# Causal mask of a latent attention added by two 64 × 64 quadrant products instead of one 128 × 128 product

## The chip, the cores and the metric

The kernel runs on one core of a Trainium2 chip. The metric is the device time of one execution in microseconds (us), taken as the median of repeated runs. A core has TensorE (PE for matmuls, PEld for its weight loads), VectorE (DVE), ScalarE (ACT), GpSimd (POOL) and SyncE (SP), which run side by side and meet only at semaphores.

## What is computed

A chain of two transformer blocks on one sequence of 512 tokens by 1024 features. The part that matters here is one sublayer of the second block, a causal latent attention with 16 heads whose queries and keys have 96 features (64 plain, 32 rotated) and whose values have 64:

```python
Q_BLOCK, MLA_HEADS, QK_NOPE, QK_ROPE, V_HEAD = 128, 16, 64, 32, 64

def causal_block_attention(q, k, v, scale):
    ...
    def one_block(args):
        qi, n = args
        s = jnp.einsum('bhqd,bhkd->bhqk', qi, kt).astype(jnp.float32) * scale
        qpos = n * Q_BLOCK + jnp.arange(Q_BLOCK)
        s = jnp.where(kpos[None, :] <= qpos[:, None], s, -jnp.inf)
        p = jax.nn.softmax(s, axis=-1).astype(vt.dtype)
        return jnp.einsum('bhqk,bhkd->bqhd', p, vt)
```

Before it run two layers of another block (attention without a mask, a gated recurrence, a convolution, an MLP) and a gated MLP; after it a gated MLP, and a last layer with dilated attention between two more gated MLPs.

## The kernel before

All engines run programs written out by hand; nothing is scheduled by a tool, so the order of the source is the order on each engine. Weight matrices come in tiles by DMA, ACT copies each tile rounded (`split_hi`, L413), DVE subtracts to get the rest (`split_lo`, L422), and PE takes three products per tile (L444, L452 or L487): high by high, high by low, low by high.

The latent attention is woven into those projections. `mla_items` (L1923) makes the work list. For two heads at a time there are three pairs, one for query blocks 0 and 2 (key widths 128 and 384), one for block 3 (width 512), one for block 1 (width 256). Each of the two heads, called A and B below (y = 0 and 1), has its own PSUM bank, `banks[4]` and `banks[5]`. So a head pair has four score groups, in all 8 × 4 = 32 groups of two heads, and 64 masked products. `mla_at` (L1952) spreads the steps of the pairs over 17 points of each of four parts; a point lies between projection products of PE, and `weave` (L2022) runs there what is due. For one pair the steps are:

- **scores**, PE, `att_pe_step` (L849): waits for `p_ready` of the pair before (its banks are then read), then writes scores into banks 4 and 5 (L857). On top of the last 128 key columns of each group it adds the mask with a second product, an identity `EYE` by the table `CAUSAL` (L859); both are parts of the tensor `fixed`. The last product of a head counts up `s_ready`.
- DVE, `att_dve_step` (L913): for head A, then for head B, waits for `s_ready` and takes the row maximum of each group (L919), then its negative scaled (L921).
- ACT, `att_act_step` (L885): exponential with row sum for A, then for B (L893), which counts up `p_ready`.
- **divide**: DVE takes reciprocals (L928) and scales A (L933), ACT scales B (L902).
- **turn**: PE transposes the probabilities (L868), ACT copies them out (L910).
- **values**: PE multiplies by the values (L878), head A into partitions 0 to 63 and B into 64 to 127 of bank 3; for the last pair of two heads DVE stores the result (L951, L953).

In three of the parts the point 12 has `query_rope`: PE rotates queries (L1989) after all turned probabilities have been copied out of bank 6.

ACT also empties the projections' banks there (L2051, L2053, L2058, L2077). Tables and operands of scores, mask and values are float32, those of the projections are the rounded float32 form. In the profile a float32 product of the source appears as two PE records, and a rounded one as one.

In the profile's forms, 96\*128 means a stationary operand of 96 rows and 128 columns; 128\*64 one of 128 rows and 64 columns. The moving operand stands behind it.

Of the kernel before, what the change touches and what calls it, by code (L numbers as in the profile page):

```python
# [14 lines left out]
P = 128  # L15
# [13 lines left out]
HEAD = 64  # L29
# [173 lines left out]
def build(nc, io):  # L203
    ctx = ExitStack()
    with ctx:
# [28 lines left out]
        EYE, ONES, SWAP, FLIP, MSWAP, CAUSAL, REVERSE = (FIX[:, i * P:(i + 1) * P] for i in range(7))  # L234
# [30 lines left out]
        banks = [ctx.enter_context(nc.psum_tensor(f"bank{i}", [P, L], F32)) for i in range(8)]  # L265

        def line(name):
            return Line(ctx.enter_context(nc.semaphore(name)))
# [26 lines left out]
        for l in range(DEPTH):  # L295
            w = io["w_in"][l]
# [6 lines left out]
            w = io["w_out"][l]  # L303
# [20 lines left out]
        for i, s in steps2:  # L324
# [3 lines left out]
            elif i == 0:  # L328
                w = io["mla_w_in_2"][0]
# [5 lines left out]
                for part in range(4):  # L335
                    q = wq[:, 4 * QK * part:4 * QK * (part + 1)].rearrange("r (h c) -> r h c", c=QK)
# [7 lines left out]
            else:  # L344
                w = io["dil_w_in_2"][0]
# [11 lines left out]
        for u, unit in enumerate(units):  # L357
# [27 lines left out]
        s_ready, nmax_ready, p_ready, pn_ready, t_ready, pt_ready, pv_ready, o_used = (line(n) for n in (  # L385
            "scores_ready", "neg_max_ready", "probs_ready", "probs_normalised", "probs_turned", "probs_t_ready",
            "heads_out_ready", "heads_out_taken"))
# [461 lines left out]
        def att_pe_step(pe, pairs_, bufs, kind, i):  # L849
            if kind == "scores":  # L850
                pe.eng.wait_ge(p_ready.sem, p_ready.next(pe, 2, lag=2))
                both = pairs_[i]["items"]
                for n in range(len(both[0]["segs"])):
                    for y in range(2):
                        q, k, c0, add = both[y]["segs"][n]
                        b, w = banks[4 + y], k.shape[-1]
                        mm = pe.eng.matmul(b[:, c0:c0 + w], q, k, start=True, stop=add is None)  # L857
                        if add is not None:
                            mm = pe.eng.matmul(b[:, c0 + w - P:c0 + w], EYE, add, start=False, stop=True)  # L859
                        if n == len(both[0]["segs"]) - 1:  # L860
                            mm.then_inc(s_ready.sem, s_ready.add())
            elif kind == "turn":
                pair, y = divmod(i, 2)
                normal = pn_act if y else pn_ready
                pe.eng.wait_ge(normal.sem, normal.next(pe))
                pe.eng.wait_ge(pt_ready.sem, pt_ready.next(pe, lag=1 if i > 2 * bufs["one"] else 2))
                for j in range(pairs_[pair]["n"] // P):
                    mm = pe.eng.transpose(turn_bank(bufs, pair, y)[:, j * P:(j + 1) * P], bufs["pr"][i % 4][:, j * P:(j + 1) * P], EYE)  # L868
                mm.then_inc(t_ready.sem, t_ready.add())
            elif kind == "values":  # L870
                pe.eng.wait_ge(pt_seen.sem, pt_seen.next(pe, 2))
                if pairs_[i]["opens"]:
                    pe.eng.wait_ge(o_used.sem, o_used.next(pe, lag=1))
                both = pairs_[i]["items"]
                for j in range(len(both[0]["v"])):
                    for y in range(2):
                        v, c0, start, stop = both[y]["v"][j]
                        mm = pe.eng.matmul(banks[3][HEAD * y:HEAD * y + HEAD, c0:c0 + P], v, turned_probs(bufs, i, y)[:, j * P:(j + 1) * P], start=start, stop=stop)  # L878
                mm.then_inc(pv_ready.sem, pv_ready.add())

        def turned_probs(bufs, pair, y):

            return bufs["pt"][y + (2 if pair >= bufs["late"] else 0)]
# [61 lines left out]
        def turn_bank(bufs, pair, y):  # L945

            return banks[2 if y and pair < bufs["one"] else 6]
# [97 lines left out]
        def mixer_pe_step(pe, l, items, step):  # L1045
# [29 lines left out]
            elif kind in ("scores", "turn", "values"):  # L1075
# [4 lines left out]
                if (kind, i) == ("values", 0):  # L1080
                    for u, j in ((z_units(l)[0], 1), (lin[("z0", l)][-1], 1)):
                        place, turn = acc_place[units[u]["tiles_at"] + j]
                        pe.eng.wait_ge(acc_free[place].sem, turn)
                att_pe_step(pe, items, gqa_bufs, kind, i)
            elif kind == "csum":
                if i == 0:
# [1752 lines left out]
```

## Time and profile before

| | |
|---|---|
| median of 3 runs | 3885.82 us (3884.37 to 3890.31) |
| the profiled execution's own time | 3884.11 us |
| its span from first to last instruction | 3882.3 us |
| PE busy | 3676.9 us, 95% |
| DVE busy | 2141.2 us, 55% |
| ACT busy | 1350.1 us, 35% |
| mean granted TensorE clock | 0.967 |
| the latent attention's stretch | about 1868 to 2032 us of the span |

Times in the rows are microseconds from the start of the span. A row of the timeline has start, length, engine, line, operation, tensors and forms; like instructions that follow each other are merged, and xN says how many records a row holds. In brackets stands how long the engine had been idle before, and what ended that wait. Ends of matmuls are modelled: a record of a 128-column float32 product shows some 0.27 us, though the next begins 0.11 us after it, so starts are compared, not ends.

### The profile page before, as it was taken

What the parts mean: (1) busy time and instruction counts of PE and PEld (TensorE: products, weight loads), DVE (VectorE), ACT (ScalarE), POOL (GpSimd) and SP (SyncE); (2) the same over time, 40 slices, a digit from 0 to 9 for tenths busy, and PEclk for the clock granted to TensorE, in tenths of its full rate; (3) what the DMA queues carried; (4) which work ended last, traced back from release to release, by engine and by line L of the source; (5) the groups of instructions that cost most, each with busy time, mean ns of one, the idle gap of its engine ahead of it and who ended that gap; (6) DMA issues with size and microseconds to landing.
All of it is one profiled execution on the core that took longest, in us unless ns stands there. A gap on an engine that the chain in (4) does not pass through costs nothing.

```text
span 3882.3 us, 48060 instructions
## 1 busy us (share of the span) xinstructions
PE 3676.9 (95%) x19016; PEld 2966.1 (76%) x19016; DVE 2141.2 (55%) x2923; ACT 1350.1 (35%) x1795; POOL 854.0 (22%) x688
## 2 busy tenths in 40 slices
PE   8888999988899999998899999999999999989999
PEld 6567888756788878887677888788878778777887
DVE  5977444487844454347567435643574554655334
ACT  4554323256332332222673222222233333332212
POOL 2200655320055526552213630000000000000000
PEclk9999999999899999998899999999999999999999
DMA  5211655421155546563224643233322122222331
GB/s 158 64 39 47 156 146 147 103 63 47 44 147 146 147 117 152 143 146 76 62 63 101 157 125 98 73 102 97 98 74 84 61 74 74 60 66 76 98 98 65
DMA packets 564250, 377.76 MB, mean 97 GB/s; under 512 B 37297, under 2 KB 561162, under 8 KB 564026
## 3 DMA queue, kind: packets, MB, share of 16 engines
q1 hardware_dynamic: 564026, 374.69, 36.6%
q8 instruction: 151, 2.47, 0.3%
q14 instruction: 73, 0.60, 0.1%
HBM read 372.45 MB, written 2.17 MB: 96 GB/s over the span
## 4 chain that ended last, share of the span: by engine, by line
PE 77%; DVE 16%; ACT 4%; issue 2%; SPq 0%; DMA 0%; ACTq 0%; DVEq 0%
PE bank L444 61%; PE bank L452 2%; DVE conv_sum L1228 2%; PE bank L487 2%; DVE w_lo L422 2%; PE bank L481 1%; DVE std L919 1%; PE bank L482 1%; PE bank L857 1%; DVE hgrn_scores L1408 1%; DVE norm_tmp L1665 1%; DVE norm_tmp L1659 1%; ACT w_hi L413 1%; DVE X L1661 1%; PE bank L2291 1%
## 5 line engine op out<-in xcount | busy, mean ns | idle before, releaser
L444 PE MATMUL bank<-H_hi,w_hi 128*128 128x512 f32 x2384 | 968.8, 406 | 5.0 <-DVE w_lo L422 1.8
L444 PE MATMUL bank<-H_hi,w_lo 128*128 128x512 f32 x2384 | 932.0, 391 | 0.0
L444 PE MATMUL bank<-H_lo,w_hi 128*128 128x512 f32 x2384 | 931.4, 391 | 0.0
L422 DVE TENSOR_TENSOR w_lo<-w_raw,w_hi 128x2048 fp32r<-128x2048 f32 (+3 forms) x285 | 663.0, 2326 | 168.0 <-ACT w_hi L413 159.2
L413 ACT ACTIVATE w_hi<-w_raw 128x2048 fp32r<-128x2048 f32 (+3 forms) x285 | 529.1, 1856 | 308.5 <-DMA w_raw<-in_ffn_w_up 131.4
L520 POOL TENSOR_TENSOR w_mod_raw<-w_mod_raw,silu_c 128x1024 f32<-128x1024 f32 x144 | 282.8, 1964 | 1344.7 <-DMA w_mod_raw<-in_w_mod 1299.4
L444 PEld LDWEIGHTS bank<-H_hi,w_hi 128*128 128x128 f32 x2384 | 448.6, 188 | 141.1 <-issue 50.0
L444 PE MATMUL bank<-U_hi,w_hi 128*128 128x512 f32 x1376 | 540.7, 393 | 3.8 <-DVE note L963 3.8
L444 PE MATMUL bank<-U_hi,w_lo 128*128 128x512 f32 x1376 | 536.1, 390 | 0.0
L444 PE MATMUL bank<-U_lo,w_hi 128*128 128x512 f32 x1376 | 536.1, 390 | 0.0
L444 PEld LDWEIGHTS bank<-H_hi,w_lo 128*128 128x128 f32 x2384 | 448.2, 188 | 96.4
L444 PEld LDWEIGHTS bank<-H_lo,w_hi 128*128 128x128 f32 x2384 | 449.5, 189 | 90.3 <-issue 6.5
L1802 DVE TENSOR_TENSOR U_hi<-silu_gate,bank 128x512 fp32r<-128x512 f32 x88 | 60.5, 688 | 511.0 <-PE bank L444 499.8
L444 PEld LDWEIGHTS bank<-U_hi,w_hi 128*128 128x128 f32 x1376 | 259.0, 188 | 58.4 <-issue 5.1
L444 PEld LDWEIGHTS bank<-U_hi,w_lo 128*128 128x128 f32 x1376 | 258.6, 188 | 54.3
L444 PEld LDWEIGHTS bank<-U_lo,w_hi 128*128 128x128 f32 x1376 | 259.1, 188 | 52.6
L1789 ACT ACTIVATE silu_gate<-bank 128x512 f32<-128x512 f32 x88 | 52.6, 598 | 705.0 <-PE bank L444 700.6
L522 POOL TENSOR_TENSOR w_mod_raw<-w_mod_raw 128x512 f32<-128x512 f32 x144 | 214.5, 1490 | 11.3
L524 POOL TENSOR_TENSOR w_mod_raw<-w_mod_raw 128x256 f32<-128x256 f32 x144 | 159.1, 1105 | 11.3
L481 PE MATMUL bank<-H_hi,w_hi 128*128 128x512 f32 x320 | 136.2, 426 | 20.9 <-ACT H_hi L1637 11.0
L816 ACT ACTIVATE mid<-bank 128x512 f32<-128x512 f32 x64 | 38.3, 598 | 297.7 <-PE bank L444 275.5
L774 DVE TENSOR_TENSOR X<-X,bank 128x512 f32<-128x512 f32 x64 | 44.0, 688 | 172.4 <-PE bank L444 171.8
(366 smaller groups left out, 4712.7 us busy)
## 6 DMA issues: line engine op xcount, KB each, us to landing
w_mod_raw<-in_w_mod SPq DMA_DIRECT2D x576, 128.0 KB, 5.7
w_raw<-in_ffn_w_gate SPq DMA_DIRECT2D x88, 512.0 KB, 4.0
w_raw<-in_ffn_w_up SPq DMA_DIRECT2D x88, 512.0 KB, 5.4
w_raw<-in_dil_w_in SPq DMA_DIRECT2D x36, 1024.0 KB, 5.0
w_raw<-in_w_mlp_in SPq DMA_DIRECT2D x32, 1024.0 KB, 5.9
w_raw<-in_w_mlp_out SPq DMA_DIRECT2D x32, 1024.0 KB, 5.4
w_raw<-in_ffn_w_down SPq DMA_DIRECT2D x32, 1024.0 KB, 5.1
w_raw<-in_w_in SPq DMA_DIRECT2D x16, 1024.0 KB, 5.6
```

What stands on the lines that cost most here:

```text
L413: act.eng.activation(WH[u % SLOTS][:, 0:n], RAW[u % SLOTS][:, 0:n], ACT.Copy).then_inc(hi_done.sem, hi_done.add())
L422: dve.eng.tensor_tensor(WL[u % SLOTS][:, 0:n], RAW[u % SLOTS][:, 0:n], WH[u % SLOTS][:, 0:n].bitcast(F32), ALU.subtract).then_inc(lo_done. ...
L444: mm = pe.eng.matmul(bank[0:m, :], w[:, k, c0:c0 + m], r[:, k, :], start=(k == 0 and i == 0), stop=(k == kt - 1 and i == 2))
L452: mm = pe.eng.matmul(bank[:, jb * m:(jb + 1) * m], r[:, k, b * P:(b + 1) * P], w[:, k, c0:c0 + m], start=(k == 0 and i == 0), stop=(k == k ...
L481: pe.eng.matmul(banks[place][0:m, :], wh[:, k], rh[:, k, :], start=(k == 0), stop=False)
L487: mm = pe.eng.matmul(banks[place][0:m, :], w[:, k], r[:, k, :], start=(k == 0 and i == 0 and not halves), stop=(k == kt - 1 and w is wh an ...
L520: pool.eng.tensor_tensor(w[:], w[:], CSIL[:, 8 * part:8 * part + 8].unsqueeze(2).to_broadcast([P, DT, P]), ALU.mult).then_inc(pool.step.se ...
L522: pool.eng.tensor_tensor(w[:, 0:4], w[:, 0:4], w[:, 4:8], ALU.add).then_inc(pool.step.sem, pool.step.add())
L524: pool.eng.tensor_tensor(w[:, 0:2], w[:, 0:2], w[:, 2:4], ALU.add).then_inc(pool.step.sem, pool.step.add())
L1228: ins = ve.scalar_tensor_tensor(CONV[t][:, c0:c1], Z[:, ZA + t, c0 + s:c1 + s], w, CONV[t][:, c0:c1], ALU.mult, ALU.add)
L1789: act.eng.activation(SG[u % 2][:], bank[:], ACT.Silu).then_inc(free.sem, free.add())
L1802: dve.eng.tensor_tensor(UH[:, t, :], SG[u % 2][:], bank[:], ALU.mult).then_inc(dve.step.sem, dve.step.add())
```

## The change

The scores of both heads of a group are now issued first. Then, for head A and after it for head B, the mask is added by two products, rows and columns 0 to 63 and rows and columns 64 to 127 of the identity, each by the 64 rows of the table that belong to it and all its 128 columns. The two halves of the table go to the two halves of the bank's partitions; the two off-diagonal quadrants of the identity, which are zero, are no longer used. Groups without a mask (the attention of the first block) run as before.

```diff
@@ -855,8 +855,15 @@ att_pe_step, kind "scores"
                         q, k, c0, add = both[y]["segs"][n]
                         b, w = banks[4 + y], k.shape[-1]
                         mm = pe.eng.matmul(b[:, c0:c0 + w], q, k, start=True, stop=add is None)
-                        if add is not None:
-                            mm = pe.eng.matmul(b[:, c0 + w - P:c0 + w], EYE, add, start=False, stop=True)
+                        if add is None and n == len(both[0]["segs"]) - 1:
+                            mm.then_inc(s_ready.sem, s_ready.add())
+                    for y in range(2):
+                        q, k, c0, add = both[y]["segs"][n]
+                        if add is None:
+                            continue
+                        c1 = c0 + k.shape[-1]
+                        for half in (slice(0, HEAD), slice(HEAD, P)):
+                            mm = pe.eng.matmul(banks[4 + y][half, c1 - P:c1], EYE[half, half], add[half, :], start=False, stop=True)
                         if n == len(both[0]["segs"]) - 1:
                             mm.then_inc(s_ready.sem, s_ready.add())
```

The lines behind it move down by seven: L866 is the new mask product, and L868 and L878 become L875 and L885. Only PE's order changes.

On PE, the pair for blocks 0 and 2 of the second two heads, in the first weave with attention, before (keys by queries are scores, `fixed` by itself is the mask):

```order
L857 MATMUL bank<-mla_keys,mla_queries 128x128 [waits probs_ready]
L859 MATMUL bank<-fixed 128x128
L857 MATMUL bank<-mla_keys,mla_queries 128x128
L859 MATMUL bank<-fixed 128x128
L857 MATMUL bank<-mla_keys,mla_queries 128x384
L859 MATMUL bank<-fixed 128x128
L857 MATMUL bank<-mla_keys,mla_queries 128x384
L859 MATMUL bank<-fixed 128x128
L444 MATMUL bank<-latent_hi,w_hi_63 128x512
```

And the same place with the change:

```order
L857 MATMUL bank<-mla_keys,mla_queries 128x128 [waits probs_ready]
L857 MATMUL bank<-mla_keys,mla_queries 128x128
L866 MATMUL bank<-fixed 64x128 x4
L857 MATMUL bank<-mla_keys,mla_queries 128x384 x2
L866 MATMUL bank<-fixed 64x128 x4
L444 MATMUL bank<-latent_hi,w_hi_63 128x512
```

Where scores and masks alternated between the heads, both scores now stand ahead of four mask products, twice, and a projection product follows.

On PE, the pair for block 1 of the first two heads, which is followed at once by the values of an earlier pair, before:

```order
L857 MATMUL bank<-mla_keys,mla_queries 128x256 [waits probs_ready]
L859 MATMUL bank<-fixed 128x128
L857 MATMUL bank<-mla_keys,mla_queries 128x256
L859 MATMUL bank<-fixed 128x128
L878 MATMUL bank<-mla_probs_t_152,mla_values 64x128 [waits heads_out_taken,probs_t_ready]
```

With the change:

```order
L857 MATMUL bank<-mla_keys,mla_queries 128x256 [waits probs_ready]
L857 MATMUL bank<-mla_keys,mla_queries 128x256
L866 MATMUL bank<-fixed 64x128 x4
L885 MATMUL bank<-mla_probs_t_152,mla_values 64x128 [waits heads_out_taken,probs_t_ready]
```

Here the four mask products of 64 columns stand directly ahead of the values' products of 64 columns. Of the 32 score groups, 8 are followed by the next score group of the same pair, 10 by values, and 14 by a product of 128 columns of something else.

## Rows read from the trace of the kernel before

**Rows 1.** The page: busy time of each engine, and the chain that ended last
```profile
PE 3676.9 (95%) x19016; PEld 2966.1 (76%) x19016; DVE 2141.2 (55%) x2923; ACT 1350.1 (35%) x1795; POOL 854.0 (22%) x688
...
PE 77%; DVE 16%; ACT 4%; issue 2%; SPq 0%; DMA 0%; ACTq 0%; DVEq 0%
```
**Rows 2.** Busy time in windows of the attention: us, busy (records), clock, DMA
```profile
1868.00:1907.00 39.00, 30.07 (x175) 22.10 (x176) 21.90 (x49) 28.33 (x60) 11.03 (x11) 0.98 0.26 56
...
sum 164.00, PE 147.98 PEld 113.21 DVE 99.94 ACT 118.94 POOL 35.51; mean PE 36.99 PEld 28.30 DVE 24.99 ACT 29.73 POOL 8.88
```
**Rows 3.** The mask's source line, L859: records, and who waited (us, times)
```profile
L859 PE MATMUL bank<-fixed x128: 272/273/291, 1870.7 to 2021.1; 128*128 128x128 f32 x128
...
  DVE std L919: 22.5, 24
```
**Rows 4.** Timeline of PE, block 1's scores and masks before a projection
```profile
1964.98 0.60 PE L857 MATMUL bank<-mla_keys,mla_queries 96*128 96x256 f32 x2
1965.42 0.39 PE L859 MATMUL bank<-fixed 128*128 128x128 f32 x2
...
1965.87 0.39 PE L444 MATMUL bank<-latent_lo,w_hi 128*128 128x512 f32 x1
```
**Rows 5.** Timeline of PE, a mask, values of 64 columns, a projection
```profile
1960.18 1.02 PE L857 MATMUL bank<-mla_keys,mla_queries 96*128 96x512 f32 x2
1961.04 0.39 PE L859 MATMUL bank<-fixed 128*128 128x128 f32 x2
1961.36 0.66 PE L878 MATMUL bank<-mla_probs_t,mla_values 128*64 128x128 f32 x8
1961.94 0.50 PE L444 MATMUL bank<-latent_hi,w_hi 128*128 128x512 f32 x1
1962.28 0.40 PE L444 MATMUL bank<-latent_lo,w_hi 128*128 128x512 f32 x1
```
**Rows 6.** Timeline of PE, two heads' scores of 64 rows in the first block
```profile
922.44 0.69 PE L857 MATMUL bank<-k_flipped,Z 64*128 64x512 f32 x1
922.44 0.69 PE L857 MATMUL bank<-Z 64*128 64x512 f32 x1
922.97 0.59 PE L857 MATMUL bank<-k_flipped,Z 64*128 64x512 f32 x1
```
**Rows 7.** Waits of PE, 1868 to 2032: us in total, times, longest
```profile
PE bank L1989 <- ACT mla_probs_t L910: 7.0, 3, 3.0
PE bank L857 <- ACT mla_probs L893: 2.6, 2, 2.1
PE bank L878 <- ACT mla_probs_t L910: 2.4, 3, 1.0
...
PE bank L444 <- ACT mla_query_rope L2053: 1.3, 1, 1.3
```
**Rows 8.** Timeline, how a 512-wide pair leads to a wait of L1989
```profile
1938.76 0.69 DVE L919 TENSOR_REDUCE std<-bank 128x1 f32<-128x512 f32 x1 [0.86 <-PE bank L859]
...
1939.84 0.69 DVE L919 TENSOR_REDUCE std<-bank 128x1 f32<-128x512 f32 x1 [0.20 <-PE bank L859]
1939.87 0.69 ACT L893 ACTIVATE mla_probs<-bank,row_stats 128x512 f32<-128x512 f32 x1
...
1940.81 0.69 ACT L893 ACTIVATE mla_probs<-bank,row_stats 128x512 f32<-128x512 f32 x1 [0.16 <-ACT mla_probs L893]
...
1943.65 1.10 PE L1989 MATMUL bank<-mla_query_rope,fixed 128*128 128x512 f32 x2 [2.04 <-ACT mla_probs_t L910]
```
**Rows 9.** Timeline of DVE and ACT in the first part, 1870 to 1908
```profile
1878.81 0.69 DVE L919 TENSOR_REDUCE std<-bank 128x1 f32<-128x512 f32 x1
...
1879.72 0.69 DVE L919 TENSOR_REDUCE std<-bank 128x1 f32<-128x512 f32 x1
...
1898.27 0.15 DVE L921 TENSOR_SCALAR row_stats<-std 128x1 f32<-128x1 f32 x1
...
1900.24 0.69 ACT L893 ACTIVATE mla_probs<-bank,row_stats 128x512 f32<-128x512 f32 x1
```

## Prediction

> **What bounds the kernel now.** I read the page first: PE is busy 95% of the span and makes 77% of the chain that ended last, so what lengthens PE lengthens the kernel unless PE is waiting anyway [rows 1]. Then the windows: the attention fills 164 us, in which PE is busy 148 us and ACT 119 us; its first 39 us have PE busy only 30 us, so there PE waits; in the 125 us behind them it is busy 118 [rows 2]. The mask's line has 128 records for 64 products, and DVE waited 24 times for it, 22.5 us in all: the row maximum starts the moment a mask is there [rows 3]. The waits of PE in the stretch are few and have names: three for L1989, two for scores, three for values, one for a projection [rows 7]. So there are two kinds of places. Where PE waits for nothing, a change counts by PE's own time. Where PE waits for the chain from scores over DVE and ACT, it counts by how late that chain becomes, and PE's extra time vanishes in the wait.
>
> **What a mask costs on PE, before and after.** A 256-column score product takes 0.44 us from start to start, so 128 columns take 0.22 us in two records [rows 4]. One mask per head is 0.22 us, two heads 0.44 us. The new form has two products for each head, of 128 moving columns each, so each alone also takes 0.22 us. They use different rows and different columns of the array. That products in different column halves run side by side is shown by the values: eight records of 128 columns take 0.66 us, which is four steps of 0.11 with the last record's 0.27 in place of its step (0.60) and 0.05 to 0.06 on top, not eight steps [rows 5]. That different row halves do so too is shown by two 64-row scores that both start at 922.44 [rows 6]. So I take 0.22 us a head again: the quadrants save nothing, since the moving columns are as many, and lose nothing in themselves.
>
> The Trainium skill has a rule against this reading, in "TensorE: Matmul & The Clock Gate", Part 3 under the mechanism: matmuls start and end strictly in program order. By that rule the second record of one quadrant would hold back the first of the other, and two heads would need five steps of 0.11 instead of four, which at 23 places adds 2.5 us to my sum. The eight records in 0.66 us go against it, so I take four steps.
>
> **What the switches cost.** This is the main term. Going from 128-column products to the values' 64-column ones: the mask that starts at 1961.04 would be through at 1961.26, the values start at 1961.36, and 0.05 us more goes at their second step, so **0.15 us to enter** [rows 5]. Going back: the values' four steps end at 1961.36 + 0.05 + 0.44 = 1961.85, and the second projection product starts at 1962.28, 0.43 us later; after a mask of full size that distance is 1965.87 − 1965.64 = 0.23 us [rows 4, 5]. So **0.20 us to leave**. Entering a form with 128 columns costs about that too: the first step of the 64-row scores is 0.53 us where 512 columns take 0.43 [rows 5, 6]. A switch from 96 to 128 rows costs nothing: score and mask follow each other at 0.86 = 2 × 0.43 [rows 5]. Nothing in this trace is 64 by 64; the bounds are 0 (no switch) and 0.20 + 0.20, and I take 0.15 in, since the new products have the values' 64 columns, and 0.20 out. Every one of the 32 groups enters. The 10 that are followed by values do not pay for leaving, since the switch there was paid before too; the other 22 pay it.
>
> **What the new order costs.** Both scores now stand ahead of A's mask. For a 512-wide pair, A's scores with mask were there after 0.86 + 0.22 = 1.08 us; now after 0.86 + 0.86 + 0.15 + 0.22 = 2.09, **1.0 us later**. B comes 0.15 us later. But DVE needs 0.91 us from one head's maximum to the next's [rows 9] and ACT 0.94 us from exponential to exponential [rows 8], and both take A first, so B's probabilities are late by about 1.0 us too, not by 0.15. For a 256-wide pair it is 0.44 + 0.15 = 0.6 us, for blocks 0 and 2 it is 0.65 (the 384-wide score) + 0.15 and the first group's 0.35, about 1.1 us. Behind the waiting DVE stand the scalings, the stores and the weight splits, all fewer than PE's work at most places.
>
> **The sum, by place.**
> - Early part, seven groups until 1900. Of PE's waits there, the one of 2.1 us for blocks 0 and 2 grows by 1.1; the 0.5 us one behind the 512-wide pair by 1.0, and the values' wait of 1.0 us behind it is the same delay and adds nothing; the 1.3 us one at the projection by 1.1 [rows 7]. The first L1989 wait, the longest with 3.0 us, does not grow: ACT got to that pair's exponential at 1900.24 though its maximum was done at 1898.42 [rows 9], so 1.0 us later is still in time. PE's switches lie inside these waits. Together 3.2 us.
> - The two other L1989 waits (2.0 us each): A's maximum ended at 1939.45 and ACT's exponential started at 1939.87, with only the short negation between them, so there is no slack to speak of [rows 8]. Each grows by 1.0, and one group's switches vanish in each. Together 2.0 us.
> - 23 groups elsewhere, PE-bound: 23 × 0.15 = 3.45 us to enter; 14 of them leave (6 to the next score group, 8 to a product of 128 columns; 9 go to values), 14 × 0.20 = 2.8 us. Together 6.25 us.
> - In the last part the projections stand closer to the pairs, and two 512-wide pairs each wait for the exponential of blocks 0 and 2. One wait is 0.5 us already [rows 7]. They grow by about 0.6 each beyond the switches. Together 1.25 us.
>
> Sum: 3.2 + 2.0 + 6.25 + 1.25 = **12.7 us**. The profiled execution took 3884.11 us, 1.7 us under the median, so 3896.8 in its terms and 3898.5 against the median of 3885.82. What a measurement of this kernel tells from no change is about 0.2%, 7.8 us.
>
> The granted clock in the stretch is 0.96 to 1.00 and I price no change of it. POOL and the DMAs have nothing in the change and simply get more time. Instruction count on PE rises by 64 products, which is nothing beside 19016 records.
>
> **Rivals.**
> - *The quadrants of one head do not overlap.* In all pairs above, the 64-row products write different banks (heads have their own) and the values' products, which share a bank, use all 128 rows. No row shows two row halves writing one bank. If they take turns there, each group costs 0.44 us more: 23 × 0.44 = 10.1 at PE-bound places, and 0.22 to 0.44 on seven chains, about 2. Sum 25 us, 3911 us. For it: no such row; against: the column halves are separate too. The Trainium skill states such a rule, in "TensorEngine Tiling (Array Packing)", Gotcha 1: different row tiles cannot access the same PSUM bank at once. No row of this trace bears it out or denies it. Chance 0.13.
> - *The late A is absorbed.* ACT and DVE are busy 73% and 61% of the stretch [rows 2], and the waits might be fixed by ACT's other work, as at the first L1989. Then only the PE-bound term is left, 6.3 us: 3892 us, slower but under what a measurement can tell. Chance 0.16.
> - *Not slower: quadrants run in half the time and switch free.* A 64-row, 64-column product would have to take one record's time, not two, and enter without a gap. Then each group saves 0.22 us, 23 × 0.22 = 5.1 us, and the late A's still cost about 4 us: 3885 us. It decides as soon as a switch costs less than 0.11 us. Against it: scores with 64 rows still come in two records of full length, and every switch in the rows costs 0.15 or more [rows 5, 6]. Chance 0.05.
> - *The change is not there.* The order shows four 64-column mask products in each of the 32 places, so I give this nothing.
>
> **How the numbers follow.** My case has 0.66. It spans 9 to 16 us (entering 0 to 0.20, waits grown by half or in full), 3895 to 3902. The range reaches down past the absorbed case, 3890, and up to the serial one, 3911; outside are the half-time case and a serial case with all its waits. Slower by over 0.2%: my case but for its lowest edge, and the serial one, 0.78. Within 0.2%: the absorbed and most of the half-time case, 0.19. Faster by over 0.2% needs more than the half-time case gives, 0.03.
>
> **What would show it.** In the profile after, a group's last score to the mask's first record should have 0.10 us more than a step, and the four mask products (eight records) should span 0.66 us, as the values' eight do; 1.1 us would be the serial rival. From the first projection product after a mask to the second it should be 0.34 us, as after the values [rows 5]. The maximum of B should follow A's by 0.91 us everywhere, with DVE waiting for the mask before A only. The two L1989 waits should be 3 us, the first one unchanged, and the wait of 2.1 us be 3.2. The stretch should be about 12 us longer and the rest of the kernel unchanged. I am wrong if the stretch grows by less than 8 us, if the mask records do not pair, or if the time comes from outside it.

## The result, and the profile after

| | before | changed |
|---|---|---|
| median of 19 runs each | 3882.68 us | 3896.26 us |
| lowest to highest | 3877.40 to 3890.31 | 3887.05 to 3904.22 |
| profiled execution, its span | 3884.11, 3882.3 | 3898.80, 3897.0 |
| ratio | | 1.0033 (95%: 1.0025 to 1.0040) |

The change is slower, by 0.25 to 0.40%; the forecast was 3898.5 us. That forecast started from 3885.82 us, the median of three runs; the median of 19 is 3.1 us lower, so the difference to compare with the forecast's 12.7 us is 13.6 us. Two executions that stand far off the rest, 5223 us of the kernel before and 13056 us of the one with the late signal, count in the medians 3881.50 and 3896.23 below but in no ratio and no difference. The page of the changed kernel, with busy time by engine and the chain that ended last:

```profile
PE 3687.6 (95%) x19144; PEld 2962.2 (76%) x19144; DVE 2141.5 (55%) x2923; ACT 1350.8 (35%) x1795; POOL 864.3 (22%) x688
...
PE 77%; DVE 16%; ACT 4%; issue 2%; SPq 0%; DMA 0%; DVEq 0%; ACTq 0%
```

Against [rows 1], PE has 128 more records and 10.7 us more busy time; DVE and ACT are where they were. POOL's 10.3 us more are no part of the change: 11.0 of them stand ahead of the attention, in the first of the windows below. The windows of the changed kernel say where the time sits (window, length, then busy time and records of PE, PEld, DVE, ACT, POOL, granted clock, DMA share, GB/s). The first ends where the attention's window of [rows 2] began; the second holds the whole attention:

```profile
0.00:1868.00 1868.00, 1742.49 (x8857) 1393.64 (x8857) 1081.11 (x1423) 689.54 (x899) 700.85 (x554) 0.96 0.44 109
1868.00:2045.00 177.00, 158.33 (x1119) 110.20 (x1118) 104.39 (x249) 120.03 (x260) 35.13 (x35) 0.98 0.23 55
2045.00:3897.00 1852.00, 1786.80 (x9173) 1458.35 (x9171) 955.99 (x1253) 541.21 (x638) 128.32 (x100) 0.97 0.31 89
```

Ahead of the attention PE has the same 8857 records and, to 0.14 us, the same busy time as before. From the first score (1870.4 in both) to the last of the values' records the kernel before took 158.1 us, the changed one 170.2: **12.05 us of the 14.7 us between the two spans lie in this stretch**, 9.3 of them as PE busy time and 2.8 as PE idle time. The granted clock is 0.98 in it in both kernels, with 6.8 us at half clock in each. The other 2.6 us come after it, where the two programs are the same.

The mask's line, now L866, with its records and who waited; [rows 3] had 128 records and 24 waits of 22.5 us:

```profile
L866 PE MATMUL bank<-fixed x256: 269/269/473, 1870.9 to 2033.2; 64*64 64x128 f32 x128
...
  DVE std L926: 33.9, 16
```

DVE now waits for A alone, less often and for longer. The mask between products of other shapes, at a place where PE waits for nothing (start, length, then what ran):

```profile
1964.76 1.88 PE L857 MATMUL bank<-mla_keys,mla_queries 96*128 96x512 f32 x4
1966.57 0.65 PE L866 MATMUL bank<-fixed 64*64 64x128 f32 x8
1967.15 0.66 PE L885 MATMUL bank<-mla_probs_t,mla_values 128*64 128x128 f32 x8
...
1971.07 0.65 PE L866 MATMUL bank<-fixed 64*64 64x128 f32 x8
1971.66 0.50 PE L444 MATMUL bank<-latent_hi,w_hi 128*128 128x512 f32 x1
1971.99 0.40 PE L444 MATMUL bank<-latent_lo,w_hi 128*128 128x512 f32 x1
```

Each switch can be read off. **In:** four score records take 1966.57 − 1964.76 = 1.81 us to the mask; four steps of 0.43 would be 1.72, so 0.09 us is the way in. **The mask:** eight records in 0.65 us, as the values' eight in 0.66. **Out to a projection:** from the mask 0.59 us, then 0.33 us to the second product where 0.23 is the step: 0.10 ahead of the first, and 0.10 behind it. **Out to values:** 1967.15 − 1966.57 = 0.58 us, where 0.44 for four steps and 0.05 for the mask's longer second step leave 0.09. That is again a switch, and the mask of full size before had it in that place too [rows 5].

How one of the two L1996 waits (L1989 before) comes about, against [rows 8]:

```profile
1943.57 0.65 PE L866 MATMUL bank<-fixed 64*64 64x128 f32 x8
1944.12 0.69 DVE L926 TENSOR_REDUCE std<-bank 128x1 f32<-128x512 f32 x1 [1.42 <-PE bank L866]
...
1945.03 0.69 DVE L926 TENSOR_REDUCE std<-bank 128x1 f32<-128x512 f32 x1
...
1945.08 0.69 ACT L900 ACTIVATE mla_probs<-bank,row_stats 128x512 f32<-128x512 f32 x1 [0.44 <-DVE row_stats L928]
...
1948.84 1.10 PE L1996 MATMUL bank<-mla_query_rope,fixed 128*128 128x512 f32 x2 [2.55 <-ACT mla_probs_t L917]
```

B's maximum follows A's by 0.91 us and has no wait of its own; ACT takes up A as soon as it can, and from there to L1996 it is 3.76 us, where it was 3.78. The chain behind A's maximum is what it was; its start is later. The waits of PE in the attention (us in total, times, longest):

```profile
PE bank L1996 <- ACT mla_probs_t L917: 7.7, 3, 2.6
PE bank L857 <- ACT mla_probs L900: 4.6, 4, 2.6
PE bank L444 <- ACT mla_query_rope L2060: 1.8, 1, 1.8
PE bank L885 <- ACT mla_probs_t L917: 1.5, 2, 0.7
PE bank L444 <- ACT mla_values L2058: 1.4, 1, 1.4
```

Against [rows 7], the score waits (L857) grew from 2.6 to 4.6 us and from two to four; one more, of 0.7 us before the scores at 1916.35, has no releaser that the profile shows. The new ones are short, and the timeline has one before a pair of 256 and one before a pair of 512 in the last part:

```profile
2014.56 1.13 PE L857 MATMUL bank<-mla_keys,mla_queries 96*128 96x256 f32 x4 [0.41 <-ACT mla_probs L900]
2026.49 1.98 PE L857 MATMUL bank<-mla_keys,mla_queries 96*128 96x512 f32 x4 [0.44 <-ACT mla_probs L900]
```

The three waits of L1996 moved from 3.0, 2.0 and 2.1 to 2.6, 2.6 and 2.6.

### The profile page after: what moved, and what is told of

It reads as the page before. It is cut to its first block, busy times and chain, and to the rows that moved or that the text cites. A ratio compares the mean times of both kernels' runs of the same rounds, so it can differ in the third digit from the quotient of the medians.

```text
span 3897.0 us, 48316 instructions
## 1 busy us (share of the span) xinstructions
PE 3687.6 (95%) x19144; PEld 2962.2 (76%) x19144; DVE 2141.5 (55%) x2923; ACT 1350.8 (35%) x1795; POOL 864.3 (22%) x688
## 4 chain that ended last, share of the span: by engine, by line
PE 77%; DVE 16%; ACT 4%; issue 2%; SPq 0%; DMA 0%; DVEq 0%; ACTq 0%
PE bank L444 61%; PE bank L452 2%; DVE conv_sum L1235 2%; PE bank L487 2%; DVE w_lo L422 2%; PE bank L481 1%; PE bank L857 1%; DVE std L926 1%; PE bank L482 1%; DVE hgrn_scores L1415 1%; DVE norm_tmp L1672 1%; ACT w_hi L413 1%; DVE norm_tmp L1666 1%; DVE X L1668 1%; PE bank L2298 1%
## 5 line engine op out<-in xcount | busy, mean ns | idle before, releaser
L522 POOL TENSOR_TENSOR w_mod_raw<-w_mod_raw 128x512 f32<-128x512 f32 x144 | 211.0, 1465 | 11.3
L524 POOL TENSOR_TENSOR w_mod_raw<-w_mod_raw 128x256 f32<-128x256 f32 x144 | 171.7, 1192 | 11.3
L481 PE MATMUL bank<-H_hi,w_hi 128*128 128x512 f32 x320 | 135.6, 424 | 22.5 <-ACT H_hi L1644 12.5
```

Of the source, the lines that this page charges most:

```text
L481: pe.eng.matmul(banks[place][0:m, :], wh[:, k], rh[:, k, :], start=(k == 0), stop=False)
L522: pool.eng.tensor_tensor(w[:, 0:4], w[:, 0:4], w[:, 4:8], ALU.add).then_inc(pool.step.sem, pool.step.add())
L524: pool.eng.tensor_tensor(w[:, 0:2], w[:, 0:2], w[:, 2:4], ALU.add).then_inc(pool.step.sem, pool.step.add())
```

## The experiments

**How small differences were compared.** Executions of one and the same kernel here spread over 13 to 21 us, and the spread goes with the mean granted clock that is recorded for each: within the kernels, 0.001 more clock goes with 2.7 us less time. Sets of 6 to 19 runs have different mean clocks. So each result below has two numbers: the ratio of medians with its interval, and the **difference at equal clock**, from one line fitted through all executions with that slope, with its standard error. For the changed kernel it is +11.3 (0.7) us. The plain difference of its medians is 13.6 us; the 12.05 us of the stretch lie between. The difference at equal clock leaves out whatever a change does to the clock itself. All nine later sets have a lower mean clock than the runs of before (0.9657 to 0.9673 against 0.9674); only for the rounded mask, 0.9657, is this clearly more than scatter. Where the two numbers lie far apart, as there, neither alone is the worth of the change.

**What the stretches say.** Most expectations name a stretch, from the first score to the last values' record. The profiled executions of the experiments had far more half clock in it than the two kernels compared, so their stretches can't be set beside 158.1 and 170.2 us as they are. At half clock PE's own work takes nearly twice as long: at 1879 us, in the changed kernel, the next product starts 1.05 us after the first of eight mask records, elsewhere 0.59 us.

```profile
1879.15 1.12 PE L866 MATMUL bank<-fixed 64*64 64x128 f32 x8
1880.20 0.80 PE L444 MATMUL bank<-latent_hi,w_hi 128*128 128x512 f32 x1
```

The last column is an estimate from this: stretch less half of its time at half clock, against the same for the kernel before. It takes off too much where PE was waiting.

| kernel | stretch, us | of it at half clock | forecast against before | estimate against before |
|---|---|---|---|---|
| before | 158.1 | 6.8 | | |
| changed | 170.2 | 6.8 | +12.7 | +12.0 |
| order alone, first | 173.7 | 27.3 | +5.3 | +5.3 |
| order alone, again | 171.1 | 20.5 | +5.3 | +6.1 |
| late signal | 171.6 | 17.1 | +6.7 | +8.4 |
| quadrants, old order | 180.8 | 23.9 | +16.9 | +14.1 |
| quadrants for B alone | 170.8 | 23.8 | +7.3 | +4.2 |
| column halves | 178.7 | 30.7 | +10.6 | +8.6 |
| heads inside quadrants | 176.3 | 13.7 | +17 or more; rival +12 | +14.8 |
| rounded mask | 157.9 | 23.9 | −6.1 or −8.6 | −8.7 |

Signs and rough sizes are the forecast ones; single values are off by up to 3 us.

### The new order with masks of full size (two times)

```diff
-                        for half in (slice(0, HEAD), slice(HEAD, P)):
-                            mm = pe.eng.matmul(banks[4 + y][half, c1 - P:c1], EYE[half, half], add[half, :], start=False, stop=True)
+                        mm = pe.eng.matmul(banks[4 + y][:, c1 - P:c1], EYE, add, start=False, stop=True)
```

(against the changed kernel)

> Both heads' scores first, then both masks, each as one full 128 by 128 product: the order of the change without its quadrants. The stretch from the first score to the last values' record was 158.1 us before and 170.2 us with the change. If mode switches are the main cost, PE-bound places lose nothing here and only the late head A counts: 0.65 and 0.86 us at two early waits and 0.65 at a third, 0.86 at two of the L1989 waits, 0.65 at two score waits of the last part, 5.3 us in all: a stretch of 163.4 us, ratio 1.0014. Rival, the order is the main cost: 168 us or more, ratio 1.0025 or more. Rival, the late A is absorbed: 158 to 160 us.

Measured: 3891.94 us against 3882.90, ratio 1.0029 (1.0019 to 1.0039), at equal clock +7.3 (0.9). Its profiled execution was hard to read. The attention's window:

```profile
1868.00:2045.00 177.00, 154.69 (x975) 116.19 (x976) 102.40 (x243) 116.65 (x255) 35.06 (x35) 0.92 0.23 55
```

The granted clock is 0.92 where the kernel before and the changed one have 0.98, so of the 15.5 us by which this stretch is longer than before, some 10 are put down to the clock by the estimate above. The kernel was run again beside the second set:

> The kernel of the first order-only run once more, for its interval and for a trace with the clock at its upper level in more of the stretch. The waits' account says 5.3 us, ratio 1.0014; the first runs say 1.0029 with an interval from 1.0019, of which their lower mean clock (0.9663 against 0.9673) explains about 2.5 us. At PE-bound groups the intervals between groups should be those of the kernel before within 0.1 us; the increase should stand at seven groups before waits.

Measured: 3888.10 us against 3881.50, ratio 1.0013 (1.0003 to 1.0023), at equal clock +4.3 (0.9). Together +5.8. The two sets ran on different chips; against the kernel before on the same chip they are +6.8 and +5.0 (0.9 each). The forecast was 5.3. Its waits of PE:

```profile
PE bank L1995 <- ACT mla_probs_t L916: 8.4, 3, 3.0
PE bank L857 <- ACT mla_probs L899: 7.6, 5, 4.6
```

The interval from each group of scores to the next, against before, is unchanged to 0.2 us at twelve places where PE waits for nothing in either kernel, and 0.56 to 1.13 us longer at five places behind 1964 us where it comes to wait. (The clock in the stretch is 0.94, but behind 1964 us each of the two kernels has just one piece of 3.4 us at half clock, in the same interval.) So the order costs nothing on PE itself and acts through the late A alone, as the prediction priced it.

### Late signal alone

PE's program is that of before to the last record; A's count of `s_ready` is moved to B's mask.

```diff
-                        if n == len(both[0]["segs"]) - 1:
+                        if n == len(both[0]["segs"]) - 1 and add is None:
                             mm.then_inc(s_ready.sem, s_ready.add())
+                        elif n == len(both[0]["segs"]) - 1 and y:
+                            mm.then_inc(s_ready.sem, s_ready.add(2))
```

> The kernel before with nothing moved and nothing added: A's count on s_ready is made by B's mask, together with B's. PE's work is the same to the record; A is late by B's score and mask, 1.08, 0.87 and 0.66 us for the three kinds of pair, somewhat more than in the order-only run (0.86, 0.65, 0.44). If lateness of A is what the order costs, the seven waits grow by 0.87 + 1.08 + 0.87 + 1.08 + 1.08 + 0.87 + 0.87 = 6.7 us: ratio 1.0017, a stretch of 164.8 us, and more than in the order-only run. Rival, the order costs by something else on PE: ratio under 1.0010.

Measured: 3896.23 us against 3881.50, ratio 1.0032 (1.0020 to 1.0044), at equal clock +9.4 (0.9), more than the order alone. The timeline of PE, DVE and ACT at one of the pairs of 512:

```profile
1940.72 0.39 PE L859 MATMUL bank<-fixed 128*128 128x128 f32 x2
...
1941.81 0.39 PE L859 MATMUL bank<-fixed 128*128 128x128 f32 x2
...
1942.30 0.69 DVE L921 TENSOR_REDUCE std<-bank 128x1 f32<-128x512 f32 x1 [1.32 <-PE bank L859]
...
1943.21 0.69 DVE L921 TENSOR_REDUCE std<-bank 128x1 f32<-128x512 f32 x1
1943.27 0.69 ACT L895 ACTIVATE mla_probs<-bank,row_stats 128x512 f32<-128x512 f32 x1 [0.34 <-DVE row_stats L923]
```

A's mask starts at 1940.72, but its maximum starts only behind B's mask, 1.09 us later than it could. B follows by 0.91. PE has nothing more to do than before and the kernel is 9.4 us slower: that a later A is paid is shown by this run without any other change. The sum over seven waits was 6.7 us, too little by three standard errors; which places make the rest was not traced. It is paid more than in the order run, which delays A by 0.86 and not by 1.09 us (0.86/1.09 of 9.4 is 7.4); the rest is within twice its error.

### Quadrants in the order of before

```diff
-                            mm = pe.eng.matmul(b[:, c0 + w - P:c0 + w], EYE, add, start=False, stop=True)
+                            for half in (slice(0, HEAD), slice(HEAD, P)):
+                                mm = pe.eng.matmul(b[half, c0 + w - P:c0 + w], EYE[half, half], add[half, :], start=False, stop=True)
```

> Quadrant products, but each head's two directly behind its own score, as the masks stood before. Twice as many switches: 64 in at 0.15 us and 54 out at 0.20 us, and head A only 0.15 us late, B 0.50 us. If switches cost what the trace before said, the 23 PE-bound groups cost 46 x 0.15 + 37 x 0.20 = 14.3 us and five waits grow by about 0.5 each, 2.5 us: a stretch of 175 us, ratio 1.0043. Rival, the order costs more than the switches: less than the change, under 170 us. Rival, the quadrants themselves are slow: the same mask records spaced by more than 0.11 us.

Measured: 3902.12 us against 3882.90, ratio 1.0050 (1.0036 to 1.0065), at equal clock +16.0 (1.1), the slowest of all, where 1.0043 was expected. Its timeline of PE shows both switches paid for each head:

```profile
1958.06 1.02 PE L857 MATMUL bank<-mla_keys,mla_queries 96*128 96x512 f32 x2
1959.01 0.44 PE L860 MATMUL bank<-fixed 64*64 64x128 f32 x4
1959.38 1.12 PE L857 MATMUL bank<-mla_keys,mla_queries 96*128 96x512 f32 x2
1960.43 0.43 PE L860 MATMUL bank<-fixed 64*64 64x128 f32 x4
1960.80 0.50 PE L444 MATMUL bank<-latent_hi,w_hi 128*128 128x512 f32 x1
```

From A's scores to B's it is 1.32 us, where a mask of full size makes 0.86 + 0.22 = 1.08 [rows 5]. A's mask starts 0.95 us after its scores (0.09 for the way in) and lasts 0.37 to B's scores (0.22 for two steps, 0.05 for the long second one, 0.10 for the way out), and B's scores need 1.05 instead of 0.95 to their mask, the other half of the way out. Given quadrants, the new order is the better one; it halves the switches.

### Quadrants for head B alone

```diff
-                            mm = pe.eng.matmul(b[:, c0 + w - P:c0 + w], EYE, add, start=False, stop=True)
+                            for half in (slice(0, HEAD), slice(HEAD, P)) if y else (slice(0, P),):
+                                mm = pe.eng.matmul(b[half, c0 + w - P:c0 + w], EYE[half, half], add[half, :], start=False, stop=True)
```

> The order of the kernel before; A's mask is one full product, only B's is two quadrants. One switch in and one out per group, as in the change, and A is not late, B by 0.15 us. The switches alone should cost 23 x 0.15 + 14 x 0.20 = 6.3 us at PE-bound places and 0.15 us at seven waits, 1 us: 7.3 us, a stretch of 165.4 us, ratio 1.0019. Rival, the switches are mostly hidden and the change's cost is the late A: a ratio under 1.0012.

Measured: 3890.47 us against 3881.50, ratio 1.0018 (1.0007 to 1.0029), at equal clock +5.6 (0.9). One way in and one out for each group, as in the changed kernel, with A's signal where it was before:

```profile
1957.88 0.39 PE L860 MATMUL bank<-fixed 128*128 128x128 f32 x2
1958.10 0.81 PE L857 MATMUL bank<-mla_keys,mla_queries 96*128 96x384 f32 x2
1958.84 0.44 PE L860 MATMUL bank<-fixed 64*64 64x128 f32 x4
1959.20 1.09 PE L879 MATMUL bank<-mla_probs_t,mla_values 128*64 128x128 f32 x16
```

384 columns have two steps of 0.32, so 0.74 us to the mask is 0.10 for the way in; and the four quadrant records take two steps, 0.36 us to the values. This run gives the switches without the order: +5.6, and 1.0019 was expected. Its interval alone would leave room for the rival, a ratio under 1.0012; the switches in its timeline, the same as in the changed kernel, do not. With the order's +5.8 the two halves make 11.4, and the changed kernel has 11.3. Each half has an error of about 1 us, so the agreement is closer than the runs can show.

### Halves by columns alone

```diff
-                            mm = pe.eng.matmul(banks[4 + y][half, c1 - P:c1], EYE[half, half], add[half, :], start=False, stop=True)
+                            mm = pe.eng.matmul(banks[4 + y][half, c1 - P:c1], EYE[:, half], add, start=False, stop=True)
```

(against the changed kernel: every product uses all 128 rows, as the values' do)

> As the change, but each mask product takes all 128 rows and 64 columns of the identity, the form of the values' products. If what costs is a switch of form, the same 0.15 us in and 0.20 us out, but the 10 groups that are followed by values now need no switch there, which saves 0.15 us each, 1.4 us in PE-bound places: ratio 1.0029 where the change has 1.0033, a stretch near 168.7 us, and 0.11 us from the last mask record to the values in place of 0.20. Rival, the cost comes with 64 rows: no switch is seen before the mask, and the ratio falls to that of the order alone.

Measured: 3896.11 us against 3881.50, ratio 1.0030 (1.0017 to 1.0043), at equal clock +11.6 (1.0), that of the changed kernel. The 1.4 us less that were expected are within the error, and the rival, a ratio near that of the order alone, is not seen. One place of its timeline of PE:

```profile
1920.31 1.03 PE L857 MATMUL bank<-mla_keys,mla_queries 96*128 96x256 f32 x4
1921.27 0.66 PE L866 MATMUL bank<-fixed 128*64 128x128 f32 x8
1921.76 1.04 PE L885 MATMUL bank<-mla_probs_t,mla_values 128*64 128x128 f32 x16
```

The way in is the same: 0.96 us for four steps of 0.22 is 0.08 more. The way to the values is free, 0.49 us instead of 0.58, since the shape stays 128 by 64. The masks of the two row halves gain nothing and lose nothing: the column halves alone set the four steps.

### Heads inside the quadrants

The order of the four mask products is A's upper, B's upper, A's lower, B's lower.

```diff
-                    for y in range(2):
-                        q, k, c0, add = both[y]["segs"][n]
...
-                        for half in (slice(0, HEAD), slice(HEAD, P)):
+                    for half in (slice(0, HEAD), slice(HEAD, P)):
+                        for y in range(2):
+                            q, k, c0, add = both[y]["segs"][n]
```

> As the change, but the four mask products in the order A upper quadrant, B upper, A lower, B lower, so that neighbours use the same quadrant. If matmuls start strictly in program order, B upper must finish queueing behind A upper before A lower can start: six steps of 0.11 us instead of four, 0.22 us more in each of 23 PE-bound groups, 5.1 us: a stretch of 175 us or more. Rival, each quadrant has its own queue: four steps as in the change, and a stretch within 1 us of 170.2 us. Head A's mask is then ready 0.1 to 0.2 us later, worth up to 1 us at the waits.

Measured: 3899.06 us against 3882.90, ratio 1.0041 (1.0025 to 1.0057), at equal clock +14.9 (1.1). PE and DVE at a pair of 512:

```profile
1942.28 0.66 PE L866 MATMUL bank<-fixed 64*64 64x128 f32 x8
1942.87 0.50 PE L444 MATMUL bank<-latent_hi,w_hi 128*128 128x512 f32 x1
...
1943.05 0.69 DVE L926 TENSOR_REDUCE std<-bank 128x1 f32<-128x512 f32 x1 [1.47 <-PE bank L866]
```

Eight records still take 0.66 us, and pairs of them start 13 to 14 ns apart (6 to 7 ns in the changed kernel): four steps, though by the source order only the two products in the middle could go together. Strict order would make seven steps; the six in the expectation are a miscount. But A's maximum starts 0.77 us after the mask's first record, where it is 0.55 in the changed kernel (1943.57 to 1944.12): two steps of 0.11 later. By the records, the one that counts up A's signal is in the second step, so A's lower quadrant starts ahead of B's upper; and DVE hears of it as if it ended behind B's upper. The 0.22 us lie on the same chain that is paid above. PE waits for ACT about a dozen times in this stretch; if each wait grew by 0.22 us, that would be 2.6 us, an estimate that no run parts from the rest. The kernel is 3.6 us behind the changed one, with an error of 1.3 us.

### The mask in rounded float32, order and size of before

Both operands of the mask product are copied once, at the start of DVE's attention program, into a rounded float32 table, and the product of before reads the copies.

```diff
+        ROUND = at("mask_rounded", small_at + 2 * P * 4, [P, 2, P], F32R)
...
-                            mm = pe.eng.matmul(b[:, c0 + w - P:c0 + w], EYE, add, start=False, stop=True)
+                            mm = pe.eng.matmul(b[:, c0 + w - P:c0 + w], ROUND[:, 0, :], add, start=False, stop=True)
...
-                            segs.append((MQ[0:QK, s, b * P:(b + 1) * P], MK[0:QK, s, 0:w], c0, CAUSAL))
+                            segs.append((MQ[0:QK, s, b * P:(b + 1) * P], MK[0:QK, s, 0:w], c0, ROUND[:, 1, :]))
...
+            for n, src in enumerate((EYE, CAUSAL)):
+                dve.eng.tensor_copy(ROUND[:, n, :], src).then_inc(dve.step.sem, dve.step.add())
+                dve.eng.wait_ge(dve.step.sem, dve.step.made)
```

> The kernel before, with identity and causal table copied once into the rounded float32 form, so that the mask is one PE record instead of two; full 128 by 128 products in the old order, no switches. If a record of 128 rounded columns takes 0.11 us (its weight load of 128 columns shows no less), each head saves 0.11 us: 46 x 0.11 = 5.1 us at PE-bound places and 0.11 to 0.2 us at seven waits, 1 us: a stretch of 152 us, ratio 0.9984. If it takes 0.055 us: 0.165 us a head, a stretch of 149.5 us, ratio 0.9978. Rival, a narrow rounded product costs as much as a float32 one: 158 us.

Measured: 3879.12 us against 3882.90, ratio 0.9989 (0.9979 to 0.9998), at equal clock −8.1 (0.9). It is the only version that beats both kernels. Its interval ends just below 1, and by the plain medians it gains 3.8 us, half of the 8.1 at equal clock: its mean clock of 0.9657 is among the lowest of all sets, and whether the shorter mask lowers it was not tested. The expected 0.9984 is in the interval, 0.9978 just outside. Its timeline of PE:

```profile
1938.31 1.02 PE L858 MATMUL bank<-mla_keys,mla_queries 96*128 96x512 f32 x2
1938.77 0.62 PE L860 MATMUL bank<-mask_rounded 128*128 128x128 f32 x1
1939.23 1.07 PE L858 MATMUL bank<-mla_keys,mla_queries 96*128 96x512 f32 x2
```

The mask is one record in place of two. A's scores and mask take 0.92 us, where they took 0.86 + 0.22: the step to B's scores fell by 0.16 us. B's scores then need 0.51 us to their mask where A's needed 0.46, so 0.05 us comes back. Per group of two heads that is 0.27 us saved (0.11 + 0.16), and at five places that neither kernel waits at the interval from one group of 128 columns to the next score group is shorter by just that. So a mask costs 0.08 to 0.09 us a head in place of 0.22. The record's own 0.62 us is a modelled end; the step to the next start is what counts.

## Why the prediction was right

**The cost of a mask.** Held. Eight records in 0.65 us, four steps. The 1.1 us that would have been the serial rival's stand at one place, 1879 us; it ran at half clock, and its records pair like all others. The rival in which two quadrants of one head take turns in their bank is refuted: they start 6 to 7 ns apart in all 32 groups. The rule of the Trainium skill that stood behind that rival ("TensorEngine Tiling (Array Packing)", Gotcha 1: different row tiles cannot access one PSUM bank at once) did not show itself in any of the 32 groups, for the two diagonal quadrants tried here.

**Program order.** The rule weighed there, from the Trainium skill's "TensorE: Matmul & The Clock Gate", Part 3, that matmuls start and end in program order, would have made five steps. The trace has four, and the run with the heads inside the quadrants parts the rule in two: starts do not keep the program's order across quadrants, while what DVE is told does.

**The switches.** Held in size at each place: 0.09 + 0.05 to enter (taken: 0.15), 0.20 to leave to a projection (taken: 0.20), 0.09 to 0.10 between mask and values, already paid before. One remark of the rival of free switches contradicts its own rows: "every switch in the rows costs 0.15 or more", where the 64-row scores show 0.53 − 0.43 = 0.10. In the intervals from one group of scores to the next, the changed kernel has, at nine places without a new wait, +0.13 to +0.22 us where values follow (three), +0.42 and +0.43 where a product of 128 columns does (two), and +0.47 to +0.68 over two groups (four). The sum had 0.15, 0.35, and 0.50 to 0.70. Two more have +0.34 (values follow, from 1923.26) and +0.58 (a projection, from 1970.12): in the order-only run the same two grew by 0.69 and 0.56 and end or hold a wait of 0.5, so the late A has a part in them. At 1995.06 it is +0.12 where 0.35 was due, and the kernel before has the end of a piece at half clock there. One interval that should have paid 0.35 paid nothing: in it the scores of 128 columns had been waiting 0.33 us longer before.

**The late A.** Held as a mechanism: the run with the late signal alone shows it without any switch. The early intervals before the first L1996 grew by 2.8 us (predicted 3.2), though one part of that term was misplaced: the wait of 0.5 us that I put there is the one at 1999 us, in the last part, so it was counted in both terms, and what stood there was the values' wait alone. The changed kernel also ran 3.4 us of this part at half clock (from 1878.9) and the kernel before none, so part of the 2.8 us may be the clock's, and that the term came out is in part luck. The two later L1996 were to grow by 1.0 us each as *waits*, to 3 us; they grew by 0.5 each. The intervals around them grew by 0.84 and 1.03, as the sum had it. I had mixed the two up: idle time behind a later chain grows by the delay less the work that now stands ahead of the wait, and B's scores, the masks and the switches stand there. For the same reason the wait of 2.1 us, forecast at 3.2, is 2.6, and that of 1.3 us is 1.8. The first L1996 wait was to stay at 3.0 us and is 2.6; its interval became 1.1 us shorter, where the kernel before ran 2.5 us of it at half clock and the changed one none. In the whole stretch both have 6.8 us at half clock, so the two places offset each other.

**The last part.** The two waits before pairs of 512 came as priced: 0.5 us became 1.17, one of 0.44 is new, and the order-only run has their intervals longer by 0.64 and 0.57 (0.6 each in the sum). What I did not see is the third wait: the pair of 256 behind the first of them now waits as well, 0.41 us, and its interval is 0.92 us longer, 1.13 in the order-only run. The wait rows of before could not show it; the distance from a pair's exponential to the next pair's scores, where PE was just in time, would have.

The sum, against the stretch:

| term | predicted | measured |
|---|---|---|
| early part, to the scores ahead of the first L1996 | 3.2 | 2.8 (3.4 us at half clock in changed) |
| interval of the first L1996 wait | 0 | −1.1 (half clock in before) |
| the two other L1996 waits | 2.0 | 1.9 |
| all other intervals: switches, and the last part's waits | 6.25 + 1.25 | 8.5 (0.9 of it the interval with the wait not foreseen) |
| sum | 12.7 | 12.05 |

By the kind of cost, the kernels with one part each give about +5.8 us for the order (7.3 and 4.3 in its two sets of runs) and +5.6 (0.9) for the switches; at equal clock the changed kernel has 11.3 (0.7). The rivals of an absorbed A (6.3 us in all) and of free switches (about 0) lie far below.

What stays open: the 2.6 us by which the two profiled executions differ behind the attention, where the programs are the same. Their place can be read: for 39 us behind the last values, PE's records keep the distances of before to 0.02 us, then within 11 us they fall 2.55 us behind, and to the end the lag stays between 2.1 and 2.6. There the changed kernel ran 13.7 us at half clock, the one before 10.2, and one wait of PE is longer, in before and in the changed kernel:

```profile
PE bank L481 <- ACT H_hi L1637: 2.1, 1, 2.1
PE bank L481 <- ACT H_hi L1644: 3.6, 1, 3.6
```

Whether this place always takes longer behind the changed attention, or only did so in this execution, one profile of each can't tell. Nor were the switches priced at half clock, or the rest of the late signal's 9.4 us traced to places.

## What to carry to other kernels

Before a product is split into parts of the array, see whether the moving columns or the records become fewer; here two quadrants of 128 columns each cost what one full product does, and entering and leaving them cost 0.14 and 0.20 us beside products of 128 columns. When a pair of results feeds a serial chain, batching "all firsts, then all seconds" delays the first by the second one's share of the stage (0.86 us here); see whose signal moves later, and by how much, before counting what the batch saves. Before cutting a small product into pieces, look at its number format: the same 128 by 128 mask in one rounded record cost 0.08 to 0.09 instead of 0.22 us a head.

## What the runs showed of the hardware that was not expected

- Products of different quadrants in one bank start 6 to 7 ns apart, and with another product of the source between them still 13 to 14 ns; the signal then came 0.22 us later, as if behind the product that was overtaken.
- A rounded 128-column product behind a float32 score adds 0.06 us to the step and, where another score follows, 0.05 us to that one's; the float32 one adds 0.22.
- A change from 96 to 128 rows at 128 columns costs nothing; from 128 columns to 64, and from 128 rows to 64 at 64 columns, each cost 0.09 to 0.10 us.
- The mean granted clock of an execution, 0.962 to 0.971 here, goes with 2.7 us for each 0.001. Two sets of the same kernel (order alone) on two chips differed by 3 us at equal clock even so, by 1.8 us when each is set against its own chip's runs of before. So a difference of 3 us or less between versions of different sets was not settled by 11 or 12 runs of each.
- The profiled executions had 6.8 to 30.7 us of half clock in a stretch of 158 to 181 us, so one stretch of two profiles compares only after a look at the clock in it.
